# All six late tiles of the last combine summed on TensorE, in a ring of four PSUM bank pairs, with smaller moves at the ends of both expert stages

## What is computed

```
def hier_moe(hn, ...):                                  # two experts per token, gates g0 and g1
    ...
    y = jnp.zeros((n + 1, d)).at[slot_tok].add(ys * slot_w[:, None])[:n]
...
    h = h + hier_moe(rmsnorm(h, norm_ffn_g[i]), ...)    # h + g0*y0 + g1*y1
return rmsnorm(h, final_norm_g)[:, N_META:]
```

## Time and profile before

| | us |
|---|---|
| median of 3 runs | 2759.39 (2759.09 to 2761.17) |
| the profiled execution's own time | 2757.82 |
| its span, from the first to the last instruction | 2756.1 |
| PE busy in it | 2468.3 (90%) |
| DVE busy | 1070.4 (39%) |
| ACT busy | 542.2 (20%) |
| moved by DMA | 567.11 MB, 206 GB/s in the mean |

### The profile page before, as it was taken

How to read it: one execution, slowest core, us unless ns; L and a number is a source line. 1 busy time by engine, 2 the same in 40 slices (tenths; PEclk the granted TensorE clock), 3 DMA queues, 4 the chain that set the end, 5 groups by cost and what they waited for, 6 DMA issues and landing times. The chain is left out here.

```text
span 2756.1 us, 39574 instructions
## 1 busy us (share of the span) xinstructions
PE 2468.3 (90%) x16337; PEld 1534.6 (56%) x16337; DVE 1070.4 (39%) x2211; ACT 542.2 (20%) x1228; POOL 347.1 (13%) x375
## 2 busy tenths in 40 slices
PE   9999988898999998987777889999999989777777
PEld 5444568547888655554444455766674555444443
DVE  3473554666455653311111154445545431111113
ACT  1312465210000011111111141322331111111112
POOL 3321102400000211111111000000003111111110
PEclk9999999999999999999999999999999999999999
DMA  3111010231013236999999980000113499999998
GB/s 118 35 38 50 23 48 5 79 115 44 33 46 119 80 127 251 422 425 425 425 425 425 398 311 21 17 24 8 56 42 138 155 402 424 424 426 425 426 424 350
DMA packets 89110, 567.11 MB, mean 206 GB/s; under 512 B 19536, under 2 KB 19696, under 8 KB 59728
## 3 DMA queue, kind: packets, MB, share of 16 engines
q1 hardware_dynamic: 63504, 506.86, 45.1%
q0 software_dynamic: 20528, 39.84, 3.8%
q10 hardware_dynamic: 4896, 17.83, 1.6%
HBM read 529.06 MB, written 66.06 MB: 216 GB/s over the span
## 5 line engine op out<-in xcount | busy, mean ns | idle before, releaser
L3267 PE MATMUL ex__h_ps<-all__arena,ex__xT 128*64 128x256 f32 x3392 | 407.1, 395 | 107.9 <-DMA all__arena<-in_w_up_t 83.8
L3267 PEld LDWEIGHTS ex__h_ps<-all__arena,ex__xT 128*64 128x64 f32 x3392 | 249.6, 142 | 277.7 <-DMA all__arena<-in_w_up_t 123.4
L3318 DVE COPY ex__ysb<-ex__y_ps 128x512 f32<-128x512 f32 x64 | 44.3, 692 | 487.1 <-PE ex__y_ps L3287 477.0
L3287 PE MATMUL ex__y_ps<-b__w,ex__hT 128*64 128x512 f32 x640 | 146.8, 600 | 26.7 <-issue 26.7
L3487 POOL DMA_INDIRECT b__rows<-s_hn,mo__queue x60 | 60.6, 1011 | 745.4 <-PE ex__x_ps L3260 745.4
L3309 DVE TENSOR_TENSOR ex__hs<-ex__sg,ex__h_ps 128x256 f32<-128x256 f32 x64 | 27.0, 422 | 304.4 <-PE ex__h_ps L3267 304.4
L2540 PE MATMUL cm__acc<-all__arena,cw__w 128*128 128x260 f32 x576 | 136.0, 386 | 2.6 <-PEq L84 2.3
L2540 PE MATMUL cm__acc<-all__arena,cm__sums 128*128 128x260 f32 x576 | 134.3, 383 | 0.0
L2540 PEld LDWEIGHTS cm__acc<-all__arena,cw__w 128*128 128x128 f32 x576 | 110.4, 192 | 20.4 <-issue 3.3
L2540 PEld LDWEIGHTS cm__acc<-all__arena,cm__sums 128*128 128x128 f32 x576 | 109.5, 190 | 17.2 <-issue 0.3
L3300 ACT COPY ex__xT<-ex__x_ps 128x512 f32<-128x512 f32 x64 | 37.5, 586 | 380.6 <-PE ex__x_ps L3260 380.6
(11 more groups left out here) (586 smaller groups left out, 4122.7 us busy)
## 6 DMA issues: line engine op xcount, KB each, us to landing
all__arena<-in_w_up_t SPq DMA_DIRECT2D x62, 2048.0 KB, 44.0
all__arena<-in_w_gate_t SPq DMA_DIRECT2D x40, 2048.0 KB, 43.5
b__w<-in_w_down_t SPq DMA_DIRECT2D x40, 2048.0 KB, 44.7
mo__wx<-in_w_gate_t SPq DMA_DIRECT2D x22, 2048.0 KB, 44.0
all__arena<-in_w_down_t SPq DMA_DIRECT2D x22, 1024.0 KB, 38.8
mo__wx<-in_w_down_t SPq DMA_DIRECT2D x20, 1024.0 KB, 44.3
all__arena<-s_ys SPq DMA_DIRECT2D x15, 1024.0 KB, 8.8
cw__w<-in_conv_w_in_t SPq DMA_DIRECT2D x24, 512.0 KB, 4.5
```

Of the source, the lines that this page charges most:

```text
L3267: last = nc.tensor.matmul(h_ps[half, c, DE * b:DE * b + DE], xT[:, b, k, half], slots[c][:, n, k], start=(k == 0), stop=(k == KT - 1))
L3287: last = nc.tensor.matmul(y_ps[half, c], hT[:, b, k, half], rows[k][:, n, 512 * c:512 * c + 512], start=(k == 0), stop=(k == 1))
L3318: return nc.vector.tensor_copy(ysb[:, b, 512:], y_ps[:, 1])
```

## The change

1. At the end of the expert stage, residual products of all early tiles but tile 0 are issued ahead of the last pair's down products (there is such a tile in the second layer only); that of tile 0 stays behind them.
2. SP loads only one tile's rows of `s_ys` behind `last_stored` inside the expert stage (before: up to `NBUF`, two tiles in either layer). The rest are loaded first thing in the next phase.
3. In the second layer, SP waits until the early rows have landed before it loads the gain and the residuals.
4. `FILL` of the first layer is 8 instead of 4, and the two unread products ahead of the first `turn` are gone.
5. In the last stage PE sums all six late tiles, in order of their numbers, in four pairs of banks; tile 6 reuses the banks of tile 2, tile 7 those of tile 3. A tile's residual products are issued ahead of the wait for its rows. DVE's three sums are gone.

```diff
@@ the expert stage, SP
                 sp.wait_ge(after.last_stored, 16)
-                for t in range(NE, after.NBUF):
-                    after.rows_in(sp, t)
+                after.rows_in(sp, NE)
@@ the expert stage, PE
+                def residual_product(t):
+                    pe.wait_ge(after.h_loaded[t], 16)
+                    for c, part_of in halves:
+                        nc.tensor.matmul(early_banks[t][:, c], ident[:], after.hb[:, t, part_of], start=True, stop=False)
+
+                for t in after.EARLY[1:]:
+                    residual_product(t)
                 pe.wait_ge(m["hT_out"], PAIRS_M)
                 ...
                 last.then_inc(m["y_done"], 1)
-                for t in after.EARLY:
-                    pe.wait_ge(after.h_loaded[t], 16)
-                    for c, part_of in halves:
-                        nc.tensor.matmul(early_banks[t][:, c], ident[:], after.hb[:, t, part_of], start=True, stop=False)
+                residual_product(0)
@@ class LatentLoads
-    FILL = 4
+    FILL = 8
@@ combine_and_latents, SP, first in its list
+                for t in range(len(pre.EARLY) + 1, NBUF):
+                    pre.rows_in(sp, t)
@@ combine_and_latents, PE
-                pe.wait_ge(q_scaled, KT)
-                for k in range(2):
-                    mm(aq[:, 1, 0:QR], wq[:, k, 0:P], wq[:, k], start=True, stop=True)
                 turn(0)
@@ class FinalLoads
     def behind_early(self, sp):
+        for t in self.EARLY:
+            sp.wait_ge(self.y_loaded[t], 16)
@@ combine_out
-        BY_PE = (2, 4, 6)
-        TURNS = (0, 1, 3, 2, 5, 4, 7, 6)
+        TURNS = tuple(range(TT))
+        BY_PE = TURNS[len(pre.EARLY):]
+        BANKS = 4
-        acc = ph.ps("acc", [P, len(BY_PE), 2, 512])
+        acc = ph.ps("acc", [P, BANKS, 2, 512])
@@ combine_out, SP
-                for t in range(NBUF, TT):
+                for t in range(len(pre.EARLY) + 1, TT):
                     sp.dma_start(yb[t], D["ys"][P * t:P * t + P]).then_inc(y_loaded[t], 16)
@@ combine_out, PE
                 for n, t in enumerate(BY_PE):
+                    b = n % BANKS
+                    if n >= BANKS:
+                        pe.wait_ge(scaled, t - BANKS + 1)
                     pe.wait_ge(h_loaded[t], 16)
+                    for c, part_of in halves:
+                        nc.tensor.matmul(acc[:, b, c], ident[:], hb[:, t, part_of], start=True, stop=False)
                     pe.wait_ge(spread_done, 2 * (n + 1))
                     pe.wait_ge(y_loaded[t], 16)
-                    for c in range(2):
-                        part_of = slice(512 * c, 512 * c + 512)
-                        nc.tensor.matmul(acc[:, n, c], ident[:], hb[:, t, part_of], start=True, stop=False)
+                    for c, part_of in halves:
                         for e in range(2):
-                            last = nc.tensor.matmul(acc[:, n, c], spread[:, n, e], yb[t][...], start=False, stop=(e == 1))
+                            last = nc.tensor.matmul(acc[:, b, c], spread[:, n, e], yb[t][...], start=False, stop=(e == 1))
@@ combine_out, DVE
-                scale(0)
-                scale(1)
-                make(3)
-                make(5)
-                scale(2)
-                scale(3)
-                make(7)
-                scale(4)
-                scale(5)
-                scale(6)
-                scale(7)
+                for n in range(TT):
+                    scale(n)
```

24 lines of the change are left out of this document (7 added, 17 removed).

## The result

| | before | changed |
|---|---|---|
| median, us (6 runs each, taken together) | 2759.24 (2757.76 to 2761.61) | 2777.55 (2775.26 to 2779.20) |
| ratio | | 1.0062 [1.0051, 1.0073] |
| the profiled execution's own time and its span, us | 2757.82, 2756.1 | 2775.26, 2773.5 |

The two medians are 18.3 us apart, and the ratio says 0.62% slower. The forecast was +10.4 us, a median of 2769.8 with a range of 2767.5 to 2772.3: the sign is right, and the measured median lies above the range.

The account below looks back on a forecast made before the run. The last stage was bound by gathered rows' landing plus a DVE/ACT tail, PE nearly as long; the latents by PE. Latents -1.3 and last stage +11.7 gave +10.4 us, median 2769.8, range 2767.5 to 2772.3.

Parts of the forecast that it names:

- latents' stretch: Latents' stage: block closes 0.3 us earlier, first turn starts 2.0 earlier; open clock gives -2.4 to +0.4, -1.3 taken.
- end of the second expert stage: Tile 1's residual product takes 1.72 us, 0.46 of it in PE's gap; the block closes 0.5 us earlier.
- last stage: PE's 36 more rows add 15.45 us; the stage ends at 2767.8 against 2756.1, +11.7.
- The signs named in the prediction: Last stage: PE runs some 33 us without waiting, DVE and ACT wait for PE, gathered rows land by about 2743.
- 17.5 us for 36 rows, the half-clock rows at its start included: Last stage: PE's time for three tiles before, kept as the base to which 15.45 us for 36 more rows is added.
- the case of a longer low clock: Last stage's start: PE's half-clock time unknown; none would be -1.9 us, a second stretch of the same length +1.9.
- The price of a row: PE in the last stage: each row costs 0.43 us, 12 rows 5.15, against the skill page's reading by LDWEIGHTS busy.
- SP's moves: Later row and residual loads cost nothing: other waits cover them, early rows load alone, residuals land by about 2724.
- the case taken: Latents' opening: the clock falls, for a gain of 1.3 us down to a loss of 0.4; -1.3 was taken.
- The second: Rival: clock low for longer in last stage (+1.9) and latents (+0.4 in place of -1.3): +14.0, 2773.4; chance 8%.
- The first: Rival: clock holds through the latents' opening, -2.4 us in place of -1.3, median 2768.7; chance 20%.
- the third: Rival: rows' landing, not PE, bounds the last stage; rows about 0.24 us apart, 2754.4, not slower; chance 4%.

Follow-up runs that it names:

- e2: Kernel before with only tile 1's residual product moved ahead of the second expert stage's last down products: stage end 25.57 us against 20.72, ratio 1.0016.
- e4: The residual move alone, reading rows long in SBUF, with the wait for the residual behind the down products: stage end 20.19 us, ratio 0.9995.
- e3: Changed kernel with tile 1's residual product put back behind the down products: stage end 20.72 us, last stage 43.94, ratio 1.0046 to before.
- e10: The residual move alone plus four unread products (8 rows) filling PE's wait: stage end 23.96 us against 20.72 before, ratio 1.0004.
- e8: Kernel before with the first layer's part alone (FILL 8, two unread products gone): latents' stretch 123.13 us against 122.22, ratio 1.0008.
- e1: Kernel before with the last stage's part alone, all six late tiles summed on PE: last stage 41.98 us against 28.74, ratio 1.0040.
- e5: Kernel before with all six late tiles on PE but without their residual products (24 rows): last stage 32.38 us, PE 22.88, ratio 1.0010.
- e11: Kernel before with four late tiles (2, 4, 6, 7) summed by PE, two by DVE: last stage 31.94 us against 28.74, ratio 1.0017.
- e7: Kernel before with only SP's moves (one tile's rows behind the scatter, wait ahead of gain and residuals): last stage 31.29 us, ratio 1.0010.
- e6: Kernel before with PE summing tiles 2, 4, 7 instead of 2, 4, 6, residual products first: last stage 28.28 us against 28.74, ratio 1.0009.

## Why the prediction was right or wrong

By stretch, forecast against measured. All are differences to before, in us; the forecast's last stage runs from 2727.36 - 0.5 to 2767.8, 40.9.

| | forecast | measured | error |
|---|---|---|---|
| latents' stretch | -1.3 | +0.34 | +1.6 |
| end of the second expert stage | -0.5 | +5.61 | +6.1 |
| last stage (28.74 before) | +12.2 | +13.81 | +1.6 |
| scatter ahead of and between them | 0 | -2.36 | -2.4 |
| span | +10.4 | +17.4 | +7.0 |

**The end of the second expert stage: the step that failed.** The prediction put tile 1's residual product into PE's gap of 0.46 us ("The residual product of tile 1 is put there: 2 products, 4 rows", "of which 0.46 falls into the gap") and asked how long its rows take, not whether its operand is there. It wasn't. The loads of the two early residuals are these (the line that issues them, second expert stage; issue times, and from issue to landing). Both, before:

```profile
L4137 SPq DMA_DIRECT2D all__arena<-s_h x2: 326/3959/7592, 2675.2 to 2675.6; - x2
...
DMA to landing us min/median/max: 34.6/35.0/35.5
```

The first of the two by itself, that of tile 0, before (window 2674 to 2675.4):

```profile
L4137 SPq DMA_DIRECT2D all__arena<-s_h x1: 326/326/326, 2675.2 to 2675.2; - x1
...
DMA to landing us min/median/max: 34.6/34.6/34.6
```

And both with the change:

```profile
L4142 SPq DMA_DIRECT2D all__arena<-s_h x2: 327/3947/7567, 2673.2 to 2673.6; - x2
...
DMA to landing us min/median/max: 34.6/35.0/35.5
```

They are issued behind the last weights, when the queues move some 425 GB/s, and land 34.6 us (tile 0) and 35.5 us (tile 1) later in both kernels. In before tile 1's residual is there at 2675.6 + 35.5 = 2711.1, and its product starts at 2713.48: the order of before had 2.4 us to spare, and tile 0's residual, there at 2709.8 and wanted at 2711.66, 1.9. A wait that is met does not stand in any list of waits. Moved into the gap, the product is wanted when the hidden transposes end, in before at 2707.11 + 0.50 = 2707.61, and 2711.1 - 2707.61 = 3.5 us is the wait that came: in the changed kernel from 2705.60 (2705.09 + 0.50) to 2709.1. All of these numbers could be read from the trace of before. e2 shows that the move alone does it, e4 that without the wait the stretch is shorter by the half microsecond forecast, e3 that it was all of this stretch, e10 that 3.2 of e2's 4.85 is the wait and 1.6 the clock. The clock's fall is in the changed kernel's windows (columns as above; the last row is from the last stage and used below):

```profile
2706.00:2707.00 1.00, 0.00 (x0) 0.00 (x0) 0.00 (x0) 0.01 (x1) 0.00 (x0) 1.00 0.75 299
...
2708.00:2709.00 1.00, 0.00 (x0) 0.00 (x0) 0.00 (x0) 0.00 (x0) 0.00 (x0) 0.50 1.03 430
...
2714.00:2715.00 1.00, 1.00 (x6) 0.28 (x4) 0.00 (x0) 0.00 (x0) 0.00 (x0) 0.99 0.00 0
2737.50:2738.00 0.50, 0.50 (x2) 0.17 (x1) 0.00 (x0) 0.00 (x0) 0.00 (x0) 0.58 0.98 410
```

Granted clock 1.00 in the microsecond after PE stopped, 0.50 two microseconds on, and full again only in the window at 2714, after 5 us of work: the 4 residual rows take 3.78 in the place of 1.88.

**The last stage: mechanism right, the term for its opening too small.** The signs named in the prediction are in the trace: PE starts on the identity 0.75 us after the stage opens (forecast 0.74), each tile takes 5.15 at full clock, the ring of four bank pairs makes no wait, ACT waits for PE before each of the six tiles (4.84 us, then 3.71 five times), and the rows land first, though at 2746.8 and not by 2743. What was too small is "17.5 us for 36 rows, the half-clock rows at its start included": it carried over 2.0 us of half-clock loss from before, and the changed kernel lost 34.24 - 6 x 5.15 = 3.3. From the first row to ACT's first squares are 8.5 us for 12 rows.

The clock was not low for longer. These windows hold its fall, before and then changed (the rises are in the earlier trace rows and above, 2737.50):

```profile
2726.00:2726.50 0.50, 0.00 (x0) 0.00 (x0) 0.00 (x0) 0.24 (x1) 0.00 (x0) 0.61 0.52 180
```

```profile
2731.00:2731.50 0.50, 0.00 (x0) 0.00 (x0) 0.39 (x2) 0.00 (x0) 0.35 (x2) 0.59 0.33 131
```

Read from the share of each window at 1.00, it was at half from 2726.1 to 2732.9 before and from 2731.1 to 2737.9 after, 6.8 us in both. Before, 3.2 us of that passed while PE waited for the rows of tile 2 and 3.7 fell on its work; after, PE had begun at 2731.70, and 6.2 fell on its work. About half of the difference (1.2 us) is the earlier start of PE against the end of its unread products (idle for 4.2 us in the place of 5.3), which the prediction made itself and did not carry into this term. The rest (1.4 us) is that the clock fell later, 3.6 us after PE had stopped and not 2.2. That part scatters: behind the same unread products it fell between 2.0 us (e8) and 5.3 us (e3) after PE had stopped. In e1, with the changed kernel's order, it fell after 2.3 us, and 5.0 us of the low clock fell on PE's work. What decides when it falls is open. The prediction named the case of a longer low clock and bounded it by +1.9; 1.3 of it came. The tail from PE's end to the span's end is 7.6, forecast 7.3.

**The price of a row.** The pace of the earlier trace rows was the right price: e5 takes 24 rows away and the stage gets shorter by 0.40 us for each, e11 adds 12 and PE's stretch grows by 4.8. LDWEIGHTS busy reads 2.19 of 5.00 us in the windows above while PE had nothing to spare. The Trainium skill, "Perfetto Trace Analysis", section "Identifying the Most-Contended Engine", judges TensorE's headroom by MFU and LDWEIGHTS busy; it calls matmul busy time no good measure of the distance to roofline, not, as the prediction puts it, one that overstates. By LDWEIGHTS busy alone the room would have seemed to be there, and in this stage the measurement is against that reading.

**Costed at nothing, SP's moves.** In the changed kernel no cost of theirs shows, but by cover: its last stage opens late against its scatter, and PE never waits for rows. Alone they cost 2.55 (e7) and, with PE's new order but without the late opening, 2.0 (e3). The reason given, "the early rows now load alone", earned 0.1 us: in e7 the scatter still waits for them. The prediction did not say what the moves cost where that cover is gone.

**The latents.** The block closes 0.3 earlier, as forecast (17.27 to 16.94), and the first turn follows the scaling. Timeline of the changed kernel, answering to the earlier trace rows:

```profile
1594.91 1.94 PE L3907 MATMUL cl__tp<-cl__ident,all__arena 128*128 128x128 f32 x8 [3.29 <-DVE all__arena L4057]
...
1597.95 7.06 PE L3921 MATMUL cl__aq<-all__arena 128*128 128x384 f32 x16 [1.10 <-ACT all__arena L3999]
```

The clock had fallen, as in the case taken, but it stayed low to the bad end of it: the turn takes 1.94, the query products 7.06 in the place of 5.43. The rise of the changed kernel's clock is inside this window (columns as above):

```profile
1601.00:1601.50 0.50, 0.50 (x2) 0.20 (x2) 0.28 (x1) 0.12 (x1) 0.00 (x0) 0.72 1.02 408
```

The query products start 3.55 earlier than in the earlier trace rows, of which 2.25 is this execution's lead from ahead of the change; the other 1.3 are spent on the 1.63 that they take longer, and +0.33 is left, the "loss of 0.4" that the prediction gave as its other end. By the earlier trace rows the two unread products that the change removes had run through most of the low clock of before, 2.7 us of the 3.4 that fell on PE's work; without them the turn and the query products take the low clock themselves. Whether it is a loss at all stays open; it is well inside the 1.2 us by which kernels with the same code here differ.

**The rivals.** The second came nearly whole in its cost, more of PE's work at the low clock at both openings: +1.3 and +1.6 over the forecast, where it had +1.9 and +1.7 and a chance of 8%. It alone, 1.3 + 1.6 on top of 2769.8, would have been 2772.7, at the range's end. The first, the clock holding in the latents, did not come (nor did its gain come in e3, where the clock held through most of the turn, 1.24 us, and then fell on the query products: 122.64), and the third, a gain because PE is not the bound, is refuted by e5 and e11. The case that took the time out of the range, a wait for tile 1's residual, was not among them. The three stretches erred by 9.4 us together, all in one direction; that the median came out only 7.8 us above the forecast, and the span 7.0, is luck, the scatter of executions being in the other direction.

## What to carry to other kernels

Before moving an instruction ahead of others, take from the trace when each of its operands lands or is written, not only what the instruction costs; a wait that is met, here by 2.4 us, does not appear in any list of waits, and a move by 5.9 us turns it into one of 3.5. Before giving the engine that bounds a stretch work that another engine does off the chain, count its rows at the pace seen there: here 12 rows, 5.15 us, bought the removal of 2.6 us of DVE work. Gains of half a microsecond ahead of a stage that waits for transfers may not arrive (e4). And when a load is delayed "because it has time", write down whose work gives it that time, since the next edit may take it away.

## What the runs showed of the hardware

A load of 0.5 MB took 34.6 to 35.5 us from issue to landing when issued behind queued weights at some 425 GB/s; stores of the same size in the last stage land after 3.7 us in the median, as this line of the tile `co__ho` of the changed kernel shows (answering to the earlier trace rows):

```profile
DMA to landing us min/median/max: 2.6/3.7/15.7
```

An idle stretch of about 3.5 us on PE cost more than itself: 1.6 us more in e2. There the granted clock fell only after PE had resumed, 4.4 us after it had stopped, so that a full clock at the first row does not say that the idle time was free. Behind the unread products at the second expert stage's end it fell between 2.0 and 5.3 us after PE had stopped, in kernels that are the same there. In the last stage 12 rows on the identity took 7.90 us at its start (e6), where 5.15 is their time at full clock: the low clock falls on PE's work instead of on its wait. Starting PE early on work that needs no gathered rows was worth less than the time by which it started early.
